# Two output products of a three-layer block, whose chunk pairs 2 to 6 are computed by seven block products with fp32 split in two

## What is computed

```python
    y = (o.astype(z.dtype) * jax.nn.silu(z)) @ w_out     # first layer
    x = x + rmsnorm(y, g_post[i])
...
        y = jnp.concatenate([a_out, c_out, m_out], axis=-1) * jax.nn.silu(gate)
        o = y @ w_o[l]                                    # layers l = 0, 1
        x = x + rmsnorm_2(o, post_norm_g[l])
```

## Time and profile before

| | |
|---|---|
| median of 3 runs | 2207.29 us |
| the profiled execution, span from first to last instruction | 2207.3 us |
| TensorE matmuls busy | 2190.0 us, 99% |
| VectorE busy | 1375.6 us, 62% |
| ScalarE busy | 815.8 us, 37% |
| GpSimd busy | 111.9 us, 5% |

### The profile page before, as it was taken

How to read it: one execution, slowest core, us unless ns; L and a number is a source line. 1 busy time by engine, 2 the same in 40 slices (tenths; PEclk the granted TensorE clock), 3 DMA queues, 4 the chain that set the end, 5 groups by cost and what they waited for, 6 DMA issues and landing times.

```text
span 2207.3 us, 27611 instructions
## 1 busy us (share of the span) xinstructions
PE 2190.0 (99%) x10348; PEld 1823.7 (83%) x10348; DVE 1375.6 (62%) x2016; ACT 815.8 (37%) x1249; POOL 111.9 (5%) x151
## 2 busy tenths in 40 slices
PE   8999999999999999999999999999999999999998
PEld 7888888888888888888888888888888888888887
DVE  6687788874248643567677732386434677677665
ACT  6433434442235421334333532345213443335221
POOL 0100001101110100000000011101000000000000
PEclk9999999999999999999999999999999999999999
DMA  7455545452247222225444432373222253435432
GB/s 280 168 157 154 163 151 159 143 186 101 97 147 268 93 96 96 76 74 158 136 140 120 167 120 95 128 272 113 98 95 74 65 158 125 144 116 159 174 118 109
DMA packets 90141, 303.05 MB, mean 137 GB/s; under 512 B 7440, under 2 KB 48656, under 8 KB 66768
## 3 DMA queue, kind: packets, MB, share of 16 engines
q1 hardware_dynamic: 83760, 270.81, 37.5%
q10 hardware_dynamic: 4896, 17.30, 2.1%
q0 software_dynamic: 1408, 13.89, 1.7%
HBM read 253.74 MB, written 48.23 MB: 137 GB/s over the span
## 4 chain that ended last, share of the span: by engine, by line
PE 95%; DVE 2%; DMA 1%; issue 1%; ACT 0%; SPq 0%; POOL 0%; DVEq 0%; POOLq 0%; ACTq 0%
PE acc L551 72%; PE sc L551 11%; PE ov L551 5%; PE ov L715 1%; PE sc L896 1%; PE sc L897 1%; PE sc L702 1%; PE sc L701 1%; DMA raw<-w_dram 1%; DMA g<-xT_dram 0%; PE acc L736 0%; PE acc L737 0%; PE acc L570 0%; PE acc L566 0%; PE acc L740 0%
## 5 line engine op out<-in xcount | busy, mean ns | idle before, releaser
L551 PE MATMUL acc<-h_hi,hi 128*128 128x512 f32 x2240 | 876.5, 391 | 8.0 <-DVE h_lo L1479 8.0
L551 PE MATMUL acc<-h_lo,hi 128*128 128x512 f32 x2240 | 873.0, 390 | 0.0
L551 PE MATMUL acc<-h_hi,lo 128*128 128x512 f32 x2240 | 872.6, 390 | 0.0
L1387 DVE TENSOR_TENSOR lo<-raw,hi 128x2048 fp32r<-128x2048 f32 (+3 forms) x178 | 390.6, 2194 | 353.1 <-ACT hi L1006 351.3
L551 PEld LDWEIGHTS acc<-h_hi,hi 128*128 128x128 f32 x2240 | 421.1, 188 | 97.7 <-issue 11.4
L551 PEld LDWEIGHTS acc<-h_hi,lo 128*128 128x128 f32 x2240 | 421.1, 188 | 88.3
L551 PEld LDWEIGHTS acc<-h_lo,hi 128*128 128x128 f32 x2240 | 421.3, 188 | 84.9
L1006 ACT ACTIVATE hi<-raw 128x2048 fp32r<-128x2048 f32 (+3 forms) x178 | 327.5, 1840 | 398.6 <-PE acc L551 256.6
L1088 ACT ACTIVATE prob<-prob,st 128x256 f32<-128x256 f32 x128 | 63.6, 498 | 109.4 <-DVE st L1540 109.4
L1020 ACT ACTIVATE sq<-acc 128x512 f32<-128x512 f32 x32 | 19.2, 600 | 224.0 <-PE acc L551 217.1
L1330 ACT ACTIVATE prob<-sc,st 128x512 f32<-128x512 f32 x64 | 44.2, 690 | 43.6 <-DVE st L1959 43.6
(11 more groups left out here) (306 smaller groups left out, 2882.6 us busy)
## 6 DMA issues: line engine op xcount, KB each, us to landing
raw<-w_dram SPq DMA_DIRECT2D x170, 1024.0 KB, 4.9
turned<-pt SPq DMA_DIRECT2D x32, 512.0 KB, 3.2
pt<-turned SPq DMA_DIRECT2D x64, 256.0 KB, 4.9
turned<-pt SPq DMA_DIRECT2D x32, 448.0 KB, 3.0
pt<-turned SPq DMA_DIRECT2D x64, 224.0 KB, 4.1
xr<-residual ACTq DMA_DIRECT2D x16, 512.0 KB, 5.1
residual<-g ACTq DMA_DIRECT2D x16, 512.0 KB, 4.7
raw<-w_dram SPq DMA_DIRECT2D x8, 896.0 KB, 6.7
```

Of the source, the lines that this page charges most:

```text
L551: ins = pe.matmul(to, a, b, start=first and n == 0, stop=last and n == 2)
L1387: dve.tensor_tensor(lo[c.slot][:, 0:width], raw[c.slot][:, 0:width], hi[c.slot][:, 0:width].bitcast(F32), ALU.subtract).then_inc(lo_done, 1)
```

## The change

In both output products the chunk pairs q = 2 to 6 (chunks 4 to 13) are computed in another way; chunks 0 to 3, 14 and 15 as before.

Of a pair (2048 rows, 256 output columns) the upper half of the rows is multiplied as before, in two half products of 8 x 3 matmuls (`half_product`, here H0 and H1, for the two column blocks). The lower half is cut in 2 x 2 blocks of rows and columns, and the tokens in two halves of 256: seven block products stand for the eight of the plain rule. They need four sums of the weight blocks, which GpSimd makes in place in `raw` and in `s_two` (`weight_sums`, `last_weight_sum`), and four sums of the activations per row tile, which GpSimd makes once per output product (`turned_sums`, 16 additions of 256 columns), and ScalarE and VectorE split (`t_hi`, `t_lo`). The weights of these chunks are packed on the host so that chunk 2q holds the four blocks of the lower half (A11, A12, A21, A22, 512 columns each) and chunk 2q + 1 the two upper halves.

A block product (`block_product`, here P1 to P7 in their order) has 4 steps. In each the high weights are multiplied by 512 columns, the 256 columns of the activations' high part and the 256 of the low part side by side, and the low weights by the 256 columns of the high part, which are added to the second half of the bank. Taking a bank out adds its two halves (`fold`, a VectorE reduction over pairs). GpSimd corrects what is taken out (`early_fixes`, `late_fixes`), and VectorE adds the half products from `acc` (L2022 and L2029 of the changed kernel) into `g`.

VectorE and ScalarE make `hi` and `lo` by units of 512 columns and halves of 1024, each as its place in the slot is read. The squares of these chunks are made later, from `g`. The memory rows are loaded by the SP queue behind P7 of the last pair, as four transfers, and scaled and split on VectorE and ScalarE behind the pairs; the angles are computed in five pieces in VectorE's part of the pairs.

The diff, cut to its core:

```diff
+            def block_product(c, bank_, unit, src, first, last):
+                for m in range(4):
+                    both = src(m)
+                    w = slice(unit.start + m * P, unit.start + (m + 1) * P)
+                    high_, low_, end = hi[c.slot][:, w], lo[c.slot][:, w], last and m == 3
+                    pe.matmul(bank(bank_).rearrange("p (s n) -> p s n", s=2), high_, both, start=first and m == 0, stop=end, skip_group_check=True)
+                    ins = pe.matmul(bank(bank_, TILES), low_, both[:, 0, :], start=False, stop=end, skip_group_check=True)
+                return ins
...
+            def out_pair(l, q):
+                c, d, no = pair_of(l, q)
+                pe.wait_ge(unit_lo, no * 6 + 3)
+                if q > Q0:
+                    pe.wait_ge(folded, no * 7 - 2)
+                block_product(c, 1, UNIT[0], y_block(0, 0), True, False).then_inc(product_done, 1)
+                pe.wait_ge(unit_lo, no * 6 + 4)
+                pe.wait_ge(t_low, l * 4 + 4)
...
+                block_product(c, 2, UNIT[1], t_block(1), True, False).then_inc(product_done, 1)
+                block_product(c, 3, UNIT[2], t_block(0), True, False).then_inc(product_done, 1)
+                pe.wait_ge(half_lo, no + 1)
+                pe.wait_ge(evacuated[c.slot], c.accs)
+                half_product(d, 0, acc[c.slot][:, :]).then_inc(half_done, 1)
+                pe.wait_ge(folded, no * 7 + 2)
+                block_product(c, 2, UNIT[3], t_block(2), False, False).then_inc(product_done, 1)
+                pe.wait_ge(unit_lo, no * 6 + 6)
+                pe.wait_ge(folded, no * 7 + 3)
+                block_product(c, 1, UNIT[2], y_block(1, 0), False, True).then_inc(product_done, 1)
+                block_product(c, 3, UNIT[0], y_block(1, 1), False, True).then_inc(product_done, 1)
+                pe.wait_ge(lo_done, c.n + 1)
+                pe.wait_ge(folded, no * 7 + 4)
+                block_product(c, 2, UNIT[1], t_block(3), False, True).then_inc(chunk_done, 1)
+                pe.wait_ge(lo_done, d.n + 1)
+                pe.wait_ge(evacuated[d.slot], d.accs)
+                half_product(d, 1, acc[d.slot][:, :]).then_inc(chunk_done, 1)
...
             def out_product(l):
-                with pe.Fori(1, KT // 2) as i:
-                    for p in range(2):
-                        features(chunk2(l, WO + p, i, 2), h_hi, h_lo)
+                for t in (2, 3):
+                    features(chunk2(l, WO + t), h_hi, h_lo)
+                for q in range(Q0, Q1 + 1):
+                    out_pair(l, q)
+                for t in (KT - 2, KT - 1):
+                    features(chunk2(l, WO + t), h_hi, h_lo)
...
+            def weight_sums(l, q):
+                c, d, no = pair_of(l, q)
+                w, s2, s1 = raw[c.slot], s_two[:, 0:SU], s_two[:, SU:2 * SU]
+                pool.wait_ge(loaded[c.slot], (c.uses + 1) * 16)
+                if q > Q0:
+                    pool.wait_ge(unit_lo, (no - 1) * 6 + 4)
+                pool.tensor_tensor(s1, w[:, A21], w[:, A22], ALU.add).then_inc(s_sum, 1)
+                pool.wait_ge(s_sum, no * 4 + 1)
+                pool.tensor_tensor(s2, s1, w[:, A11], ALU.subtract).then_inc(s_sum, 1)
+                pool.tensor_tensor(w[:, A21], w[:, A11], w[:, A21], ALU.subtract).then_inc(s_sum, 1)
...
-                pool.dma_start(area[:, :], memT).then_inc(memory_in, 16)
-                add_squares(sqacc, sq_no(l, POSTN), KT)
+                pool.wait_ge(chunk_done, chunk2(l, WO + 1).n + 1)
+                for m in range(4):
+                    turned_sums(l, m)
+                add_first_squares(sqacc, sq_no(l, POSTN))
+                weight_sums(l, Q0)
+                for t in (2, 3):
+                    add_square(sqacc, t + sq_no(l, POSTN), t % 2)
+                last_weight_sum(l, Q0)
+                for q in range(Q0, Q1 + 1):
+                    no = pair_of(l, q)[2]
+                    early_fixes(no)
+                    if q > Q0:
+                        for t in (2 * q - 2, 2 * q - 1):
+                            add_square(sqacc, t + sq_no(l, POSTN), t % 2)
+                    if q < Q1:
+                        weight_sums(l, q + 1)
+                    late_fixes(no)
+                    if q < Q1:
+                        last_weight_sum(l, q + 1)
...
+            def fold(to, b):
+                dve.tensor_reduce(to, bank(b).rearrange("p (s n) -> p n s", s=2), AX.X, ALU.add).then_inc(folded, 1)
```

More of the change, by code:

```diff
@@ L126, in build @@
     SPLIT_AT = (0, 1, 3, 4, 6, 7, 9, 10)
+    SU, TW, TILES = 512, 2048, S // 2
+    Q0, Q1 = 2, KT // 2 - 2
+    NP = Q1 - Q0 + 1
+    M_FIRST = (2, 3, 0, 1, 4, 5, 6, 7)
     def sq_no(l, which):
@@ new lines, in y_block, with t_block, half_product @@
+            def y_block(odd, tokens):
+                both = h_all[:, :].rearrange("p (s t h n) -> p s t h n", s=2, t=KT, h=2)
+                return lambda m: both[:, :, KT // 2 + 2 * m + odd, tokens, :]
+            def t_block(j):
+                return lambda m: t_part(t_parts, m)[:, j]
+            def half_product(d, n, to):
+                for k in range(KT // 2):
+                    w, x = slice(HALF[n].start + k * P, HALF[n].start + (k + 1) * P), tile(k)
+                    ins = passes(to, hi[d.slot][:, w], lo[d.slot][:, w], h_hi[:, x], h_lo[:, x], k == 0, k == KT // 2 - 1)
+                return ins
@@ new lines, in first_half, with made_square @@
+            def first_half(l, q):
+                c, d, no = pair_of(l, q)
+                act.wait_ge(loaded[d.slot], (d.uses + 1) * 16)
+                if q > Q0:
+                    act.wait_ge(half_done, no)
+                else:
+                    act.wait_ge(chunk_done, d.n - 1)
+                act.activation(hi[d.slot][:, HALF[0]], raw[d.slot][:, HALF[0]], ACT.Copy).then_inc(half_hi, 1)
+            def made_square(l, t):
+                c = chunk2(l, WO + t)
+                act.wait_ge(evacuated[c.slot], c.accs + 1)
+                square(g[:, tile(t)], t + sq_no(l, POSTN), t % 2)
@@ L1159, in output @@
             def output(l):
+                split(chunk2(l, WO + 2))
                 output_tile(l, 0, 0, chunk2(l, WO), None)
[L1161 to L1167, removed]
+                output_tile(l, 1, 1, chunk2(l, WO + 1), chunk2(l, WO + 3))
@@ L1168, in output @@
+                split(chunk2(l, WO + KT - 2))
+                for t in (KT - 4, KT - 3):
+                    made_square(l, t)
                 if l == 0:
@@ new lines, in unit_low, with half_low @@
+            def unit_low(c, unit, src, count, signal):
+                if count is not None:
+                    dve.wait_ge(unit_hi, count)
+                else:
+                    dve.wait_ge(hi_done, c.n + 1)
+                dve.tensor_tensor(lo[c.slot][:, unit], src, hi[c.slot][:, unit].bitcast(F32), ALU.subtract).then_inc(signal, 1)
+            def half_low(d, n, no):
+                if n == 0:
+                    dve.wait_ge(half_hi, no + 1)
+                else:
+                    dve.wait_ge(hi_done, d.n + 1)
+                part = HALF[n]
+                dve.tensor_tensor(lo[d.slot][:, part], raw[d.slot][:, part], hi[d.slot][:, part].bitcast(F32), ALU.subtract)\
+                    .then_inc((half_lo, lo_done)[n], 1)
@@ L2129 @@
         w2 += memory + out
-        w2 += [chunk(col(wo, P * c)) for c in range(16)] if l == 0 else sum((wide(wo[:, 512 * c:512 * (c + 1)], 4) for c in range(4)), [])
+        w2 += out_chunks(wo) if l == 0 else sum((wide(wo[:, 512 * c:512 * (c + 1)], 4) for c in range(4)), [])
     w2 = np.stack(w2, axis=1)
```

276 lines of the change are left out of this document (233 added, 43 removed).

## The result

The changed kernel takes 2213.04 us (median of 11 runs, 2211.78 to 2213.94), the kernel before 2207.38 (11 runs beside them): ratio 1.0024, 95% interval 1.0016 to 1.0033. It is 5.7 us slower; 2211 us was forecast. By the prediction's own line of 0.2% this is slower (chance 0.44), not the same (0.32), though the interval holds the line too.

The account below looks back on a forecast made before the run. TensorE, busy 99% at full clock, was taken as the bound. From 2207.3 us, 11.7 saved, 9.2 of first-pair waits and 3.2 + 2.7 of later waits gave +3.4: 2211 us, range 2199 to 2224 (8 of 10).

Parts of the forecast that it names:

- the prediction's own line of 0.2%: Whole kernel: changes within 0.2% (4.4 us, 2202.9 to 2211.7) count as the same; chances faster 0.24, same 0.32, slower 0.44.
- What TensorE saves: Output products' changed pairs: 20.59 us each instead of 21.76, so ten pairs save 11.7 us.
- The first pair of a layer: First P1 of each layer: TensorE waits about 4.6 us for low parts behind GpSimd's held token sums, twice 9.2.
- the sum: Main case, whole kernel: -11.7 + 9.2 + 3.2 + 2.7 = +3.4 us, 2211 us; chance 0.52.
- The pairs behind it: Later new pairs: waits at P1 of 0.5 us (1.2 in the second pair), P7 about 2.0; layers 3.2 and 2.7.
- The ring: Middle pairs: correction, weight sums, low parts and raw-buffer load take 21.1 us; TensorE reaches the next P1 at 20.6.
- Rival C: First P1 of each layer: the 4.6 us wait slows TensorE's clock, once or twice 2.6 us; 2214 to 2216; chance 0.12.
- A: GpSimd sums: holds matter little or the short add takes 0.45 to 0.6 us; 2196 to 2201 us; chance 0.20.
- B: VectorE folds cost more than a plain reduction; at 1.22 us each the kernel takes 2225 us; chance 0.08.
- D: Pairs' raw-buffer loads: the chunk's load takes 5.5 to 7 us beside the second; 2215 to 2227 us; chance 0.08.
- The end of a layer: Behind the last pair: loading and normalising the memory rows, 13 us of VectorE, costs nothing.
- The start of the sum: Base of the forecast: the profiled execution's span of 2207.3 us, taken to equal the median of the runs (2207.29).

Follow-up runs that it names:

- e3: Changed kernel plus three VectorE additions of 1024 columns with two SBUF operands per output stage, behind the first three token lows: 2217.84 us, ratio 1.0046.
- e4: Changed kernel plus three VectorE reductions over 1024 columns with a single SBUF operand per output stage, behind the first three token lows: 2213.61 us, ratio 1.0026.
- e2: Changed kernel with the 16 token sums of each output stage on VectorE, between its token lows, instead of on GpSimd: 2206.10 us, ratio 0.9992.
- e1: Changed kernel plus 14 throwaway matmuls of 512 columns ahead of the first block product in each output stage: 2214.54 us, ratio 1.0032.
- e5: Changed kernel with VectorE's folds of P6 and P7 moved ahead of the first low parts of the next pair's weights: 2210.61 us, ratio 1.0015.
- e7: Changed kernel with the token sums on VectorE and the folds of P6 and P7 ahead of the next pair's low parts: 2202.12 us, ratio 0.9975.

## Why the prediction was right, and where it wasn't

**What TensorE saves.** 20.59 us a pair was forecast, 20.79 measured; 9.7 us saved instead of 11.7. The short matmul was right, 117 ns in the block products for 120. The long one beside it steps 236 ns, not 226.7, and the half products take 5.46 us, not 5.44. "The two-block moving operand costs nothing extra by the nearest row" rested on durations of overlapping matmuls (391 and 392 ns), which the same paragraph had called no measure of the pace. Whether those 9 ns come from the operand or from the change of length wasn't tried.

**The first pair of a layer.** 4.6 us forecast, 4.24 and 3.93 measured, from the right cause: 0.74 us for the addition, with holds. e3 and e4 show the holds, e2 that GpSimd's row of sums is what the first block product waits for. This step was right, 1.0 us too large in the sum, and is most of the loss.

**The pairs behind it.** 3.2 + 2.7 = 5.9 us forecast, 3.1 + 3.4 = 6.5 measured, but made otherwise. The ring was described link by link with 21.1 us; it takes 21.7 to 21.8. From the P1 of 1359.90 on, the links agree up to the fourth sum (4.0 us); the last low parts end at 9.1 instead of 8.4, since the two rows of 1366.18 take 2.80 us instead of some 1.3 beside GpSimd's two square sums, a hold that the prediction did not count there. In the sum each pair waits 0.5 or more; in the trace two of the eight later P1 wait, 0.84 and 0.86, P7 waits 0.7 instead of 2.0, and 3.7 us are slow matmuls, which the sum did not have. So 5.9 came near 6.5 with other parts. It is no mere luck, since the clock's loss stands where waits would have been: in e1, with no slow matmul, the pairs lose 7.2.

**Rival C.** The clock did fall, twice, for 2.3 and 1.4 us instead of 2.6. It was an addition to the sum, at 2214 to 2216, and that step was false: time TensorE loses upstream of a ring of other engines is taken off its waits there. The chance of 0.12 for the clock's fall was too low: all eight waits of 3.9 us and more (two each in the changed kernel, e3, e4 and e5) ended in it. The time was none the worse for it.

**The others.** A (holds matter little) fell by e3; B by folds of 0.69 us; D by loads of 4.7 to 4.9 for the buffer that is waited for (the second load of the first pair takes 7.4 and 7.6, and nobody waits for it), though its case isn't empty: in layer 1 of e2 and e7 that load took 6.1 and 5.8. The end of a layer cost nothing, as said: from the first memory product to the last of the attention's values of the layer 611.31 us became 611.04.

**The start of the sum.** "The profiled execution's span of 2207.3, which equals the median of the runs": it equals it only because that run was 1.8 us above the median. With -9.7 and +14.7 from the median, and 0.45 outside the span, the sum is 2212.8. The forecast's 2211 owes some of its nearness to errors that cancel: the saving was 2.0 us too large and the first waits 1.0 too large.

## What to carry to other kernels

When a bound engine gets less work, look for a ring among the others (buffer freed, load, sums, low parts, the next free) and compare its period with the bound engine's new one; if it is longer, gains elsewhere (a cleared wait, a faster clock) come back as waits in it, until the ring is cut. A place where an engine idles ahead of a late operand is the place for whatever stands behind that operand in its queue: two folds moved there, with the token sums on the engine that does them in 0.42 us, turned +5.7 us into -5.4. Compare spans with spans and medians with medians, and read the pace of matmuls from start to start, never from their durations.

## What was not expected of the hardware

A half-clock stretch behind a wait of 3.9 to 4.3 us cost 1.4 us in some layers and 2.3 to 2.5 in others (the changed kernel 2.3 and 1.4, e5 1.4 and 2.5); waits of 1.8 us were followed by none. Behind the waits of 3.9 to 6.9 us in the changed kernel, e3, e4 and e5 the clock stayed at one half for either 3.4 or 6.8 us. At half clock a long and a short matmul step 0.64 us together, exactly their columns at 1.2 GHz; at full clock 0.353, which is 0.033 more than their columns at 2.4. And the time outside the profiled span is not a constant of the chip: 1.8 or 2.25 us, by kernel.
